# Two-layer pooling and attention decoder in full precision: the third row of output weights taken at the fifth and sixth granule of layer 1's out-projection

## The reference

```
layer 0:  h = rms_norm(x, norm0);   u, z = split(h @ w_in0)
          y = pool_mixer(u, w_pool0, pool_scale0) * silu(z)
          x = x + y @ w_out0
layer 1:  h = rms_norm(x, norm1);   q, k, v, z = split(h @ w_in1)
          q, k = rope(rms_norm(heads(q), q_norm1)), rope(rms_norm(heads(k), k_norm1))
          o = causal attention over 256 tokens, 16 heads of 128
          x = x + (o * silu(z)) @ w_out1
```

## Time and profile before

| | us |
|---|---|
| median of 3 runs (lowest, highest) | 426.38 (426.24, 426.8) |
| the profiled execution, its own time | 427.27 |
| its span, first to last instruction | 425.3 |
| PE busy in the span | 416.2 (98%) |
| DVE busy | 292.3 (69%) |
| ACT busy | 237.0 (56%) |
| mean granted TensorE clock | 0.992 of full |

### The profile page before, as it was taken

The page is one execution under the profiler, slowest core; times in us unless marked ns, Lnnn a source line. Parts: engine busy times, 40 slices in busy tenths (PEclk is TensorE's granted clock), DMA queues, the critical chain, the costliest instruction groups (busy, mean ns, idle before and its releaser), DMA issues.

```text
span 425.3 us, 5551 instructions
## 1 busy us (share of the span) xinstructions
PE 416.2 (98%) x2126; PEld 356.1 (84%) x2126; DVE 292.3 (69%) x373; ACT 237.0 (56%) x430; POOL 31.9 (8%) x45
## 2 busy tenths in 40 slices
PE   9999999999999999999999999999999999959997
PEld 8989898988888888888888888888888888848885
DVE  3879987779885545358934799358983699833532
ACT  5755453535454443469639785379846797443310
POOL 0175000000000000111001100011001010000000
PEclk9999999999999999999999999999999999988999
DMA  8996868453555747337694567794877927861002
GB/s 269 387 353 213 262 217 322 180 205 114 195 197 168 224 124 222 117 105 241 247 331 119 182 209 236 248 299 147 269 214 215 323 95 272 290 205 50 0 2 99
DMA packets 45945, 86.78 MB, mean 204 GB/s; under 512 B 2528, under 2 KB 8288, under 8 KB 45920
## 3 DMA queue, kind: packets, MB, share of 16 engines
q1 hardware_dynamic: 45200, 85.37, 60.4%
q10 hardware_dynamic: 720, 1.07, 0.8%
HBM read 79.61 MB, written 6.82 MB: 203 GB/s over the span
## 4 chain that ended last, share of the span: by engine, by line
PE 89%; DVE 6%; DMA 3%; SPq 0%; issue 0%; ACT 0%; DVEq 0%
PE acc L633 23%; PE acc L635 23%; PE acc L634 23%; PE acc L656 3%; PE acc L678 3%; PE acc L677 3%; PE acc L675 3%; DMA between<-uT 2%; DVE w_lo L848 2%; PE acc L697 1%; PE aux L688 1%; PE aux L772 1%; PE aux L779 1%; PE aux L771 1%; PE aux L790 1%; PE aux L791 1%
## 5 line engine op out<-in xcount | busy, mean ns | idle before, releaser
L848 DVE TENSOR_TENSOR w_lo<-raw,w_hi 128x2048 fp32r<-128x2048 f32 x65 | 147.9, 2285 | 45.2 <-ACT w_hi L384 45.2
L384 ACT ACTIVATE w_hi<-raw 128x2048 fp32r<-128x2048 f32 x64 | 122.0, 1914 | 43.9 <-PE acc L635 31.0
L633 PE MATMUL acc<-w_hi,hT_hi 128*128 128x512 f32 x320 | 126.9, 397 | 0.0
L635 PE MATMUL acc<-w_hi,hT_lo 128*128 128x512 f32 x320 | 124.8, 390 | 0.0
L634 PE MATMUL acc<-w_lo,hT_hi 128*128 128x512 f32 x320 | 124.6, 389 | 0.0
L635 PEld LDWEIGHTS acc<-w_hi,hT_lo 128*128 128x128 f32 x320 | 60.1, 188 | 12.9
L634 PEld LDWEIGHTS acc<-w_lo,hT_hi 128*128 128x128 f32 x320 | 60.2, 188 | 11.9
L633 PEld LDWEIGHTS acc<-w_hi,hT_hi 128*128 128x128 f32 x320 | 60.1, 188 | 11.7
L633 PE MATMUL acc<-w_hi,aT_hi 128*128 128x512 f32 x160 | 64.7, 404 | 4.9 <-DVE aT_lo L1067 4.9
L634 PE MATMUL acc<-w_lo,aT_hi 128*128 128x512 f32 x160 | 63.2, 395 | 0.0
L635 PE MATMUL acc<-w_hi,aT_lo 128*128 128x512 f32 x160 | 63.1, 395 | 0.0
(11 more groups left out here) (126 smaller groups left out, 452.1 us busy)
## 6 DMA issues: line engine op xcount, KB each, us to landing
raw<-in_w_in_dram SPq DMA_DIRECT2D x46, 1024.0 KB, 6.7
raw<-in_w_out_dram SPq DMA_DIRECT2D x16, 1024.0 KB, 5.3
raw<-in_w_pool_dram SPq DMA_DIRECT2D x4, 1024.0 KB, 5.4
between<-wide SPq DMA_DIRECT2D x8, 512.0 KB, 3.9
raw<-in_w_in_dram SPq DMA_DIRECT2D x8, 256.0 KB, 7.5
wide<-between SPq DMA_DIRECT2D x16, 128.0 KB, 2.8
qkT<-between SPq DMA_DIRECT2D x16, 128.0 KB, 2.9
between<-uT SPq DMA_DIRECT2D x3, 512.0 KB, 10.0
```

Source lines behind the costliest of these rows:

```text
L384: act.activation(w_hi[:, slot, :], raw[:, slot, :], ACT.Copy).then_inc(hi_made, 1)
L633: pe.matmul(a, shi, whi, start=first and k == 0, stop=False)
L635: ins = pe.matmul(a, slo, whi, start=False, stop=last and k == GK - 1)
L848: dve.tensor_tensor(w_lo[:, slot, :], raw[:, slot, :], w_hi[:, slot, :].bitcast(F32), ALU.subtract).then_inc(w_split, 1)
```

## The change

The table of the out-projection takes row block 2 of the weights later, and two places in the loops of ACT and DVE move.

```
-OUT1_ORDER = [(0, 0), (0, 1), (0, 2), (1, 0), (1, 1), (1, 2), (0, 3), (1, 3)]
+OUT1_ORDER = [(0, 0), (0, 1), (1, 0), (1, 1), (0, 2), (1, 2), (0, 3), (1, 3)]
...
                 if 1 <= j <= HPG:
                     probs_out(last, j - 1)
-                if j == 1:
+                if j == 2:
                     y1_hi(last - 1)
...
                 if j < HPG:
                     head_max(last, j)
-                if j == 1:
-                    y1_lo(last - 1)
                 if j == 5:
                     y1_lo_bank(last, 0)
                 if j >= 2:
                     head_out(last, j - 2)
                 n = N_OUT1 + 3 + j
                 if n < N_END:
                     weight_lo(n, n % RING)
+                if j == 2:
+                    y1_lo(last - 1)
```

## The result

| | before | after |
|---|---|---|
| median of 4 runs each (lowest to highest), us | 426.59 (426.24 to 427.39) | 419.94 (419.81 to 420.08) |
| the profiled execution, its own time | 427.27 | 419.89 |
| its span | 425.3 | 417.9 |
| mean granted TensorE clock in it | 0.992 | 0.999 |

The ratio is 0.9842, with a 95% interval of 0.9825 to 0.9859: the change is 6.65 us faster. In a second comparison it was 0.9836 (0.9815 to 0.9857).

The account below looks back on a forecast made before the run. PE, busy 98% of the span, was taken to bound the kernel; the wait (5.03 us) and slow matmuls (2.35) sum to 7.38 us, so 426.38 - 7.38 = 419.0 us in the median, range 417.9 to 420.6.

Parts of the forecast that it names:

- The wait goes: Out-projection on PE: granule 2 no longer waits for y1's low parts, starting at 375.90 instead of 380.93, gaining 5.03 us.
- The slow matmuls go: Granule 2's 18 matmuls run at full clock, 4.08 us instead of 6.43, gaining 2.35 us.
- Granule 3, granule 4 and the moved parts: No wait at either granule; y1's parts are ready at 386.3, PE wants them at 390.15, 3.9 us to spare.
- The cover that was named: Both moved pieces lie in idle time of ACT and DVE: cost none; 1.3 us at most without that cover.
- The one landing that was only bounded: Granule 5's weights, loaded ahead of the store of y1, have landed by 374.6, before ACT makes their high part.
- More changes of half cost nothing: Order of halves on PE changes five times instead of three: cost taken as zero, upper bound 0.2 us.
- Against the profiled execution's own time: Whole kernel: the profiled execution's 427.27 us less 7.38 gives 419.89.
- The median: Whole kernel: 426.38 less 7.38 gives a median of 419.0 us, the profiled execution lying 0.89 above the median.
- Rival B: Low clock around granule 2 cost more than the slow matmuls show: gain 8.4 us, 418.0 us; chance 3%.
- A: A shorter wait at granule 4 or in a step of attention: 420 to 421 us, or 423; chance 7%.
- C: Wait moves to granule 4 and grows through a late landing of y1: slower, 428.7 us; chance 1%.
- D: Granule 2 meets another hidden wait, as weights or banks: within 0.2% of before; chance 1%.

Follow-up runs that it names:

- Experiment 2: Kernel before with 21 extra unused matmuls (4.8 us at full clock) filling PE's wait ahead of granule 2: 425.0 us, ratio 0.9961.
- Experiment 7: The change with the low parts of y1 one step later on DVE (step 3): 421.24 us.
- experiment 9: Kernel before, old table; move of y1 issued before the loads of granules 4 and 5, its parts made earlier on ACT and DVE: 420.04 us, ratio 0.9852.
- experiment 1: The changed kernel run again unaltered, beside fresh runs of the kernel before: 419.98 us against 426.93 us.
- experiment 6: The change's loops of ACT and DVE, but row block 2 of half 0 at the fourth granule instead of the fifth: 425.28 us.
- experiment 3: Kernel before with 10 extra unused matmuls (2.3 us) filling about half of PE's wait ahead of granule 2: 426.0 us, ratio 0.9966.

## Why the prediction was right, and where it was off

*The wait goes*: right. The profile shows granule 2 at 375.92 (forecast 375.90).

*The slow matmuls go*: right in the profile, 4.08 us for the 18 matmuls. Experiment 2 shows the price by itself: 2.26 us between profiled executions and 1.9 between medians, against the 2.35 forecast. The prediction saw no reason for the clock to fall elsewhere, and up to PE's last matmul it did not.

*Granule 3, granule 4 and the moved parts*: right. ACT 383.31 (383.29), DVE 384.94 (385.00), PE 390.17 (390.15). The cover that was named held: both engines were idle behind the parts. Experiment 7 shows that nothing else protects this place. The one landing that was only bounded, that of granule 5's load, held too: ACT began its w_hi at 376.85 without a wait.

*More changes of half cost nothing*: right. Granule 3 to 4, a change of half in the new order, starts like granule 2, at the usual distance, and the change with its five changes (419.98) and experiment 9 with the old table's three (420.04) agree within 0.1 us.

*Against the profiled execution's own time*: 419.89 forecast, 419.89 measured. The agreement to the last digit is luck. Both profiled executions happened to reach granule 0 at the same time (363.32 and 363.35); the profiled one of experiment 1 reached it 0.74 us later and took 420.64.

*The median*: 419.0 forecast, 419.94 measured, which lies within the range given (417.9 to 420.6), and the gain of medians was 6.65 us instead of 7.38. The step that was off is the last one of the sum, "That execution lies 0.89 above the median of the runs, so for the median I forecast 426.38 - 7.38". It took the 0.89 us for an offset that both kernels share. The runs show that it was, at least in the main, part of what the change removes: before, the low clock and the landing behind the wait differ from run to run, and the profiled execution was one of those with the lower mean clock; after, there is neither, and all 4 runs lie within 0.27 us. For the gain of a median the median wait and its clock count. Experiment 2 splits that of its own comparison, 6.95 us, into 425.0 - 419.98 = 5.0 for the wait and 426.93 - 425.0 = 1.9 for the clock, so it seems to be the clock's term (forecast at 2.35) that was larger in the profiled execution than in the median one. That term is known from medians only to between 0.4 and 2.9 us, so the share of the two is not shown.

*Rival B*, 8.4 us, by the formula of the Trainium skill ("TensorE: Matmul & The Clock Gate", Terms): wrong here. The gain in the profiled executions was 7.38, and the two executions began the stage 0.03 us apart. So the throttled time that fell into the wait cost nothing here; only what was left of it when PE resumed did.

*Rivals A, C and D* did not come. C's mechanism is real, as experiment 6 shows with another table.

## What to carry to other kernels

When an engine waits for one late operand, first look whether the table of work lets it do something else in the meantime: here a changed order of the table was worth the same as a repaired queue with the parts taken earlier, and needed nothing else. When a transfer is moved up in a queue, what it passes comes late, and a consumer in strict order in front of the gain can eat most of it. A saving read from one profiled execution belongs to that execution; if the removed wait hangs on a DMA and on the clock, expect the kernel before to scatter more than the kernel after, and don't carry the profiled execution's distance from the median over to the kernel after.

## What the runs showed of the hardware

The price of the same idle time varies. Behind a wait that engine work fixed (3.16 us in the one traced execution), the low clock (1.2 GHz) cost 0, 1.4 or 2.6 us, in 2, 4 and 5 runs of 12; the twelfth fits none of these. Behind 2.65 us in the profiled run of experiment 3 it did not come, yet in 6 of its 12 runs it did; behind 0.96 us it did not in any of 6. In the kernel before (4.87 us in its traced execution) it came in 47 of 48 runs, and in those the mean clock took just two values, 0.992 and 0.996, about 1.6 us apart in time.

A store of 512 KB took 9.6 to 11.0 us in nine traces in which two loads of 1 MB each were issued just ahead of it, and 2.6 and 2.7 us in the two traces in which it was issued before them.
